# Attention queries turned once per pair and split behind the turn, in a two-layer hybrid backbone on one core

## The chip, the cores and the metric

The kernel runs on one core of one Trainium2 chip. The metric is the device time of one execution in microseconds (us), the median of three runs. One further execution was taken by the hardware profiler, and all rows below come from it.

## What is computed

Two layers of a hybrid backbone (pooling, attention, gated DeltaNet) run over 1,024 latent tokens and 128 context tokens. The change is in the attention, of which the reference says:

```
s = jnp.einsum('bqkgd,bskd->bkgqs', qblk, k, preferred_element_type=jnp.float32) * scale
p = jax.nn.softmax(s, axis=-1).astype(v.dtype)
return jnp.einsum('bkgqs,bskd->bqkgd', p, v)
```

There are 8 query heads of 64 channels and 2 key heads (4 query heads share one). Latent queries attend to 1,024 latent and 128 cached context keys, context queries to the 128 context keys alone. Each layer ends with the output projection of the gated branches, a norm and a residual.

## The kernel before

**Tiling.** `attention` works on nine pairs. Pair 0 is all context queries; pairs 1 to 8 are two heads by 512 latent queries (`PAIRS`). The inner loop has one step per pair and key tile of 128 keys, 73 steps in a layer (`ATTN_STEPS`): one for pair 0, nine for each other pair. `BASE[p]` is the first step of pair p: 0, 1, 10, 19, 28, 37, 46, 55, 64.

**A step.** TensorE computes the scores of the *next* step (`scores(n + 1)`: L1901 with the high part of the queries, `QH`, and L1902 with the low part, `QL`, for two heads), then the small items of the step's slot, then the weighted values of this step (`weighted_values`, L1911). ScalarE takes two exponentials per step (L1736), GpSimd adds them up (`add`, L1670).

**The split.** A query in float32 is a high part, rounded to float32r, and the remainder, the low part. Row 64 of `QL` holds a query's maximum over the keys and meets a row of -1 in `KO`, so that the scores come out with the maximum taken off.

**How queries get there.** A pair is handled in two halves ("asks"). For each, GpSimd's `split` copies the queries twice, rounded, into `qhh` (L1653) and subtracts to get `ql` (L1656). Item `hi`: TensorE turns (transposes) four blocks of `qhh` into PSUM bank 7 (L1811), and ScalarE copies them to `QH` (L1712). Items `max`: TensorE multiplies a block of 128 queries with all 1,152 keys (L1858, three products), VectorE reduces to a maximum per query, a column of `ql` (L1940), eight times per pair. Item `lo`: TensorE turns `ql` with its column of maxima (L1840), ScalarE copies it to `QL` (L1712). That is 16 turned blocks per pair.

**Bank 7** is also where the sums of exponentials land (`sum`, L1876) and where the DeltaNet output is turned (`o`, L1884). Each user waits until the one before has been read out (`turn_start`).

**The order** is written by hand. `attention_slots` puts the items in slots, one per step, and all engines follow it: `slots[23]` is done by each engine in step 23. Inside a slot `rank` sorts. `first` is what goes ahead of the loop, and the first four `hi` items ride in the DeltaNet scan (`QUERY_TURNS`: after scan steps 8, 10, 12, 14). VectorE also has `recip` (reciprocals, L1950), `norm` (L1958), `gate` (L1981, both inputs in SBUF), and `oscale` (scaling of `of`, L1990, both in SBUF). In the loop:

```
for n, items in enumerate(steps):
    if n + 1 < len(ATTN_STEPS):
        scores(n + 1)
    for item in items:
        work(item)
    weighted_values(n)
```

`project_out` loads the blocks of the output weights when the last `lo` is turned (six of them) and when the last scores are done (two).

## Time and profile before

| | us |
|---|---|
| median of three runs (1728.01 to 1728.64) | 1728.17 |
| the profiled execution | 1731.49 |
| its span on the core | 1729.7 |
| attention loop, layer 0, from the second score of step 1 to the first product of the projection | 580.0 to 793.0 |
| the same loop in layer 1 begins about 824 us later | |
| TensorE's mean granted clock, of full speed | 0.984 |

A row of the timeline gives the start and duration of an instruction or of a run of alike ones; "idle before" in brackets, with what ended it. Line numbers are of the kernel before. The start of the next row on an engine, less its own, is what an instruction costs there, since durations of pipelined products overlap.

### The profile page before, as it was taken

How to read it: one execution, taken by the hardware profiler on the slowest of the kernel's cores; microseconds unless marked ns; L12 is line 12 of the kernel's file. 1: busy time of each engine (PE TensorE's matmuls, PEld its weight loads, DVE VectorE, ACT ScalarE, POOL GpSimd, SP SyncE). 2: the span in 40 equal slices, each digit the busy share in tenths (PEclk: the TensorE clock that was granted, in tenths of full speed). 3: DMA queues.
4: the chain of work that ended last, by engine and by line, in shares of the span. 5: the costliest groups of instructions: out<-in, count | busy, mean ns of one | idle time of the engine just before them, and what ended most of it. 6: DMA issues, size and time to landing. Idle time of an engine off the chain costs nothing. (4 is left out here: it accounts for less than half of the span.)

```text
span 1729.7 us, 40122 instructions
## 1 busy us (share of the span) xinstructions
PE 1637.1 (95%) x17250; PEld 1343.1 (78%) x17250; DVE 1001.0 (58%) x1471; ACT 621.3 (36%) x1260; POOL 924.0 (53%) x854
## 2 busy tenths in 40 slices
PE   4899999989998999999999999998999899999998
PEld 2788999978997655556879999997899765555586
DVE  2664243827774777779238513382777477777911
ACT  4411231124444444455234123112444444445511
POOL 1000389029992587885320047911999358788532
PEclk9899999999999999999999999999999899999999
DMA  9345312210000000113321211231000000010422
GB/s 340 137 159 172 105 32 89 80 62 16 16 4 12 14 13 27 34 36 136 123 89 38 64 39 51 62 102 60 22 17 4 12 14 13 20 40 21 152 95 77
DMA packets 69776, 112.37 MB, mean 65 GB/s; under 512 B 9824, under 2 KB 41824, under 8 KB 69600
## 3 DMA queue, kind: packets, MB, share of 16 engines
q1 hardware_dynamic: 69136, 109.62, 18.8%
q8 instruction: 138, 2.26, 0.5%
q14 instruction: 38, 0.31, 0.1%
q10 hardware_dynamic: 464, 0.17, 0.0%
HBM read 90.30 MB, written 19.47 MB: 63 GB/s over the span
## 5 line engine op out<-in xcount | busy, mean ns | idle before, releaser
L1670 POOL TENSOR_TENSOR attn_accp<-attn_accp,attn_pr 128x1024 f32<-128x1024 f32 x110 | 269.4, 2449 | 42.9 <-ACT attn_pr L1736 37.2
L94 PE MATMUL ps<-in_h_hi,in_w_hi 128*128 128x384 f32 x720 | 244.1, 339 | 2.5 <-DVE in_h_lo L615 2.5
L96 PE MATMUL ps<-in_h_hi,in_w_lo 128*128 128x384 f32 x720 | 242.4, 337 | 0.0
L1940 DVE TENSOR_REDUCE attn_ql<-ps 128x1 f32<-128x1152 f32 x128 | 172.5, 1355 | 102.3 <-PE ps L1858 102.0
L1736 ACT ACTIVATE attn_pr<-ps 128x512 f32<-128x512 f32 x292 | 158.7, 595 | 170.7 <-PE ps L1902 161.8
L1901 PEld LDWEIGHTS ps<-attn_QH,attn_KH 128*128 128x128 f32 x292 | 55.5, 190 | 122.1 <-ACT attn_pr L1736 55.2
L94 PEld LDWEIGHTS ps<-in_h_hi,in_w_hi 128*128 128x128 f32 x720 | 135.7, 188 | 9.3 <-issue 7.5
L1911 PE MATMUL ps<-attn_pr,z 128*64 128x512 f32 x520 | 139.5, 615 | 0.0
L1144 POOL TENSOR_TENSOR delta_ML<-delta_EK,local 128x256 f32<-128x256 f32 x180 | 130.4, 746 | 15.2 <-PE ps L1184 14.5
L96 PEld LDWEIGHTS ps<-in_h_hi,in_w_lo 128*128 128x128 f32 x720 | 135.5, 188 | 0.0
L1901 PE MATMUL ps<-attn_QH,attn_KH 128*128 128x512 f32 x292 | 131.5, 450 | 0.0
L95 PE MATMUL ps<-in_h_lo,in_w_hi 128*128 128x384 f32 x384 | 129.6, 338 | 0.0
L94 PE MATMUL ps<-in_w_hi,in_h_hi 128*128 128x256 f32 (+1 forms) x432 | 124.2, 288 | 0.0
L1184 PE MATMUL ps<-delta_TR,delta_ML 64*64 64x64 f32 x2880 | 111.0, 223 | 13.7 <-POOL delta_ML L1144 7.9
L95 PE MATMUL ps<-in_w_lo,in_h_hi 128*128 128x256 f32 (+1 forms) x432 | 122.4, 283 | 0.0
L1902 PE MATMUL ps<-attn_QL,attn_KO 65*128 65x512 f32 x292 | 116.2, 398 | 0.0
L1184 PEld LDWEIGHTS ps<-delta_TR,delta_ML 64*64 64x64 f32 x2880 | 97.5, 137 | 20.8 <-DVE delta_TR L1430 11.7
L1430 DVE TENSOR_TENSOR delta_TR<-delta_TR,ps 128x256 f32<-128x256 f32 x180 | 72.7, 404 | 53.1 <-PE ps L1184 51.3
L1354 ACT ACTIVATE delta_X<-ps 128x256 f32<-128x256 f32 x180 | 68.8, 382 | 64.4 <-PE ps L1184 60.4
L1858 PE MATMUL ps<-attn_KH,attn_QH 128*128 128x384 f32 x384 | 89.6, 341 | 2.0 <-DVE attn_ql L1940 2.0
L1184 PE MATMUL ps<-delta_X,delta_TR 64*64 64x64 f32 x2304 | 86.4, 222 | 1.4 <-issue 0.7
L931 ACT ACTIVATE in_gate<-ps 128x384 f32<-128x384 f32 x48 | 23.4, 492 | 174.6 <-PE ps L96 93.7
(308 smaller groups left out, 3857.0 us busy)
## 6 DMA issues: line engine op xcount, KB each, us to landing
in_w<-in_w_in SPq DMA_DIRECT2D x21, 1024.0 KB, 5.1
z<-in_w_mod SPq DMA_DIRECT2D x8, 2048.0 KB, 8.0
gates<-in_gate SPq DMA_DIRECT2D x48, 192.0 KB, 1.9
attn_gt<-gates SPq DMA_DIRECT2D x34, 256.0 KB, 2.6
z<-in_x_sample SPq DMA_DIRECT2D x16, 512.0 KB, 6.0
zz<-in_w_mod SPq DMA_DIRECT2D x4, 2048.0 KB, 13.4
out_w<-in_w_out SPq DMA_DIRECT2D x16, 512.0 KB, 5.7
out_y<-z SPq DMA_DIRECT2D x16, 512.0 KB, 2.9
```

The lines of the kernel that those rows point to most:

```text
L94: nc.tensor.matmul(out, a_hi(i), b_hi(i), start=(i == 0), stop=False)
L95: nc.tensor.matmul(out, a_hi(i), b_lo(i), start=False, stop=False)
L96: last = nc.tensor.matmul(out, a_lo(i), b_hi(i), start=False, stop=(i == n - 1))
L1144: nc.gpsimd.tensor_tensor(pairs(ML[d][:, i % 2]), EA[d][:, j % 3, :, 0], level_mask(i, d), ALU.mult).then_inc(ml_done, 1)
L1184: last = nc.tensor.matmul(heads(bank, off)[rows(c), h, :], lhs(rows(c), h), rhs(rows(c), h), start=True, stop=True)
L1670: nc.gpsimd.tensor_tensor(acc, a, pr[:, n % 4], ALU.add).then_inc(pool_added, 1)
L1736: nc.scalar.activation(pr[:, n % 4, e], ps[:, e, :], ACT.Exp, scale=HD ** -0.5).then_inc(p_done, 1)
L1858: last = nc.tensor.matmul(ps[:, bank + c, 0:GRP], QH[:, p % 3, blk // 2, col:col + P], KH[:, g, GRP * c:GRP * c + GRP], start=True, stop=True)
L1901: nc.tensor.matmul(ps[:, e, :], KH[:, g, ks], QH[:, p % 3, e, :], start=True, stop=False)
L1902: nc.tensor.matmul(ps[:, e, :], KO[0:HD + 1, g, ks], QL[0:HD + 1, p % 2, e, :], start=False, stop=True).then_inc(st_done, 1)
L1911: nc.tensor.matmul(ps[HD * e:HD * e + HD, 2 + p % 2, :], values(p, kt, e), pr[:, n % 4, e], start=(kt == 0), stop=(kt == STEPS_OF[p] - 1)) ...
L1940: nc.vector.tensor_reduce(ql[:, a % 4, blk, HD:HD + 1], ps[:, bank:bank + 3, 0:GRP], AX_XY, ALU.max).then_inc(mx_read, 1)
```

## The change

- A pair's queries are turned once, as they lie, from `z` (item `turn`, four blocks of 128 by 128, both heads of the pair in one block). ScalarE rounds each head out of bank 7 into `QH` (`high`, half of the partitions each), then copies each half to the other half of the partitions (`double`). VectorE subtracts, bank 7 less `QH`, into `QL` (`lows`, two instructions of 64 by 512). These are spread over four slots: `turn` with the first `high`, `second`, `low` with the first `double`, and the second `double`.
- GpSimd's `split`, the buffers `qhh` and `ql`, and the items `hi` and `lo` are gone.
- The eight maxima of a pair are columns of a small tile `mx`. Item `row` turns all eight at once (128 by 8), ScalarE copies them to `mrow` (8 by 128) and issues a DMA from its own queue that writes them as one row of 1,024 into row 64 of `QL`. The first score of the pair waits for that DMA (`row_in`).
- In the scan there are two turns (after steps 8 and 13) and two `lows` on VectorE (after 11 and 17). Two `max` items of pair 2 move from the slots to between the scores of step 0 and of step 1.
- The `o` items 3 to 8 move from slots 14, 16, ..., 24 to slots 16 to 21.
- `QL` has three buffers in place of two, the SBUF layout moves with it, and seven blocks of the output weights are loaded once the scores of step 63 are done, the eighth after the last scores.

```diff
def attention_slots():
...
-    first += [("max", 1, 0, b) for b in range(4)] + [("max", 1, 1, 0), ("lo", 0, 0), ("max", 1, 1, 1), ("lo", 0, 1), ("max", 1, 1, 2),
-                                                     ("lo", 1, 0), ("max", 1, 1, 3), ("lo", 1, 1), ("hi", 2, 0)]
+    first = [("max", 0, 0, None), ("max", 0, 1, None)] + [("max", 1, 0, b) for b in range(4)]
+    first += [("row", 0), ("turn", 2), ("max", 1, 1, 0), ("max", 1, 1, 1), ("low", 2), ("max", 1, 1, 2), ("max", 1, 1, 3), ("row", 1)]
+    between = [("max", 2, 0, 0), ("max", 2, 0, 1)]
     slots = [[] for _ in range(len(ATTN_STEPS) + KT_LAT)]
     for p in range(2, len(PAIRS)):
         b = BASE[p]
         for i in range(4):
-            slots[b - 11 + i + (p == 2)].append(("max", p, 0, i))
+            if ("max", p, 0, i) not in between:
+                slots[b - 11 + i + (p == 2)].append(("max", p, 0, i))
             slots[b - 7 + i + (p == 2)].append(("max", p, 1, i))
-        slots[b - 8].append(("hi", p, 1))
-        slots[b - 6 + (p == 2)].append(("lo", p, 0))
-        slots[b - 2].append(("lo", p, 1))
+        slots[b - 3 + (p == 2)].append(("row", p))
         if p >= 3:
-            slots[b - 12].append(("hi", p, 0))
+            slots[b - 15].append(("turn", p))
+            slots[b - 14].append(("second", p))
+            slots[b - 13].append(("low", p))
+            slots[b - 13].append(("double", p, 0))
+            slots[b - 12].append(("double", p, 1))
     for p, b in enumerate(BASE):
         end = b + STEPS_OF[p] - 1
         at = end + (1 if p == 0 else 3)
@@ -1510,12 +1513,13 @@
         slots[at + 6].append(("gate", p))
     for t in range(NT):
         slots[5 + 2 * t].append(("oscale", t))
-        slots[8 + 2 * t].append(("o", t))
+        slots[8 + 2 * t if t < 3 else 13 + t].append(("o", t))
     for n, (k, i) in enumerate(EXTRA_GATES):
         slots[23 + 3 * n].append(("gate", k, i))
     slots[1].append(("osum",))
-    rank = {"max": 0, "recip": 2, "norm": 3, "gate": 3, "osum": 4, "oscale": 5, "hi": 6, "lo": 7, "sum": 8, "o": 9}
-    return first, [sorted(s, key=lambda x: rank[x[0]]) for s in slots]
+    rank = {"low": 0, "max": 1, "row": 2, "recip": 2, "norm": 3, "gate": 3, "osum": 4, "oscale": 5, "turn": 6, "second": 6, "double": 7,
+            "sum": 8, "o": 9}
+    return first, between, [sorted(s, key=lambda x: rank[x[0]]) for s in slots]
 
 
...
-    rc, QL = sb("rc", [P, 2, QB]), sb("QL", [P, 2, 2, QB], F32R)
-    qhh, ql, ck = sb("qhh", [P, 4, 4, P]), sb("ql", [P, 4, 4, HD + 2]), sb("ck", [P, NKV * HD])
+    QL = sb("QL", [P, 3, 2, QB], F32R)
+    mx, mrow, ck = sb("mx", [P, 3, 2, 4]), sb("mrow", [8, P], F32R), sb("ck", [P, NKV * HD])
+    row_in = [sem(f"row_in{i}") for i in range(3)]
+    for item in [("turn", 0), ("turn", 1)] + first + [x for s in slots for x in s]:
...
         sp.wait_ge(kv_out, 32)
 
     def gpsimd(pool):
-        def split(p, i):
-            n = ASKS.index((p, i))
-            if n >= 4:
-                is_turned(pool, "hi", *ASKS[n - 4])
-                is_turned(pool, "lo", *ASKS[n - 4])
-            q = queries(p, i)
-            if n < 4:
-                pool.wait_ge(q_high, n + 1)
-            for e in range(2 if n >= 4 else 0):
-                nc.gpsimd.tensor_copy(blocks(qhh[:, n % 4, :, HD * e:HD * e + HD], p).bitcast(F32R), q)
-            if n >= 4:
-                pool.drain()
...
             nc.scalar.activation(dst, src, ACT.Copy, scale=scale).then_inc(turn_copied, 1)
 
         def evict(item):
-            if item[0] == "hi":
-                _, p, i = item
-                copied(item, query_columns(QH[:, p % 3], p, i), turned_columns(slice(0, P), p))
-            elif item[0] == "lo":
-                _, p, i = item
-                r = slice(0, HD + 1)
-                copied(item, query_columns(QL[r, p % 2], p, i), turned_columns(r, p))
+            def high(p, e):
+                nc.scalar.activation(of_head(QH, half(e), p, e), turned_queries(p, e), ACT.Copy).then_inc(q_high, 1)
+
+            def double(p, e):
+                act.wait_ge(q_high, 2 * p + 2)
+                nc.scalar.activation(of_head(QH, half(1 - e), p, e), of_head(QH, half(e), p, e).bitcast(F32), ACT.Copy).then_inc(q_ready, 1)
+
+            if item[0] == "turn":
+                p = item[1]
+                is_turned(act, *item)
+                high(p, 0)
+                if p < 3:
+                    high(p, 1)
+                    double(p, 0)
+                    double(p, 1)
+            elif item[0] == "second":
+                high(item[1], 1)
+            elif item[0] == "double":
+                double(*item[1:])
+            elif item[0] == "row":
+                p = item[1]
+                is_turned(act, *item)
+                if p:
+                    act.wait_ge(row_in[(p - 1) % 3], 16 * ((p - 1) // 3 + 1))
+                nc.scalar.activation(mrow[:], ps[0:8, 7, 0:P], ACT.Copy).then_inc(turn_copied, 1)
+                act.wait_ge(turn_copied, turn[item] + 1)
+                act.dma_start(QL[HD:HD + 1, p % 3].rearrange("p e (t c) -> p (e t) c", c=P).bitcast(F32),
+                              mrow[:].bitcast(F32)).then_inc(row_in[p % 3], 16)
             elif item[0] == "sum":
                 p = item[1]
...
         if s in KEY_TURNS:
             key_turn(pe, KEY_TURNS.index(s))
         if s in QUERY_TURNS:
-            query_turn(pe, *ASKS[QUERY_TURNS.index(s)])
+            query_turn(pe, QUERY_TURNS.index(s))
+
+    def lows(dve, p):
+        dve.wait_ge(q_high, 2 * p + 2)
+        for e in range(2):
+            last = nc.vector.tensor_tensor(of_head(QL, slice(0, HD), p, e), turned_queries(p, e),
+                                           of_head(QH, half(e), p, e).bitcast(F32), ALU.subtract)
+        last.then_inc(turn_copied, 1)
+
+    def early_lows(dve, s):
+        if s in EARLY_LOWS:
+            lows(dve, EARLY_LOWS.index(s))
     def tensor(pe, out, nxt):
         def work(item):
-            if item[0] == "hi":
-                query_turn(pe, *item[1:])
-            elif item[0] == "lo":
-                _, p, i = item
-                n = ASKS.index((p, i))
+            if item[0] == "turn":
+                query_turn(pe, item[1])
+            elif item[0] == "row":
+                p = item[1]
                 turn_start(pe, item)
-                pe.wait_ge(mx_read, call_number[p, i, None if p == 0 else 3] + 1)
-                for blk in range(4):
-                    last = nc.tensor.transpose(ps[0:HD + 1, 7, P * blk:P * blk + P], ql[:, n % 4, blk, 0:HD + 1], m["ident"])
-                last.then_inc(turned, 1)
+                pe.wait_ge(mx_read, call_number[p, 1, None if p == 0 else 3] + 1)
+                nc.tensor.transpose(ps[0:8, 7, 0:P], mx[:, p % 3].rearrange("p e t -> p (e t)"), m["ident"]).then_inc(turned, 1)
             elif item[0] == "max":
                 _, p, i, blk = item
                 n, g = call_number[p, i, blk], i if p == 0 else PAIRS[p][1]
                 bank = call_bank(n)
-                is_turn_copied(pe, "hi", p, i)
+                pe.wait_ge(q_ready, 2 * p + 2)
                 if n < 2:
...
@@ -1893,13 +1890,14 @@
                 pe.wait_ge(ones_done, 1)
                 pe.wait_ge(k_copied, len(K_BANKS))
             if kt == 0:
-                is_turn_copied(pe, "lo", p, 1)
+                is_turn_copied(pe, "turn", p)
+                pe.wait_ge(row_in[p % 3], 16 * (p // 3 + 1))
             for e in range(2):
                 if n >= 1:
                     pe.wait_ge(p_done, 2 * (n - 1) + e + 1)
                 g = groups(p)[e]
                 nc.tensor.matmul(ps[:, e, :], KH[:, g, ks], QH[:, p % 3, e, :], start=True, stop=False)
-                nc.tensor.matmul(ps[:, e, :], KO[0:HD + 1, g, ks], QL[0:HD + 1, p % 2, e, :],
+                nc.tensor.matmul(ps[:, e, :], KO[0:HD + 1, g, ks], QL[0:HD + 1, p % 3, e, :],
                                  start=False, stop=True).then_inc(st_done, 1)
 
         def weighted_values(n):
...
-        for item in first[4:-1]:
+        for item in first:
-        work(first[-1])
+        for item in between:
+            work(item)
...
-QUERY_TURNS = (8, 10, 12, 14)
+QUERY_TURNS = (8, 13)
+EARLY_LOWS = (11, 17)
...
-        attn["queries_turned"](sp)
-        for k in range(6):
+        attn["last_pair_begun"](sp)
+        for k in range(KD - 1):
             w_block(k)
         attn["scores_done"](sp)
-        w_block(6)
-        w_block(7)
+        w_block(KD - 1)
         attn["values_done"](sp)
```

At three places the order on an engine is worth seeing. The first is VectorE from the end of the scan to slot 2 (`attn_ql` and `attn_mx` take the maxima, `attn_QL` is the low part), the change against before:

```order
-L1937 TENSOR_REDUCE attn_ql<-ps 128x4 x2
-L1940 TENSOR_REDUCE attn_ql<-ps 128x1 x10
+L1822 TENSOR_TENSOR attn_QL<-ps,attn_QH 64x512 x2
+L1934 TENSOR_REDUCE attn_mx<-ps 128x4 x2
+L1938 TENSOR_REDUCE attn_mx<-ps 128x1 x6
+L1822 TENSOR_TENSOR attn_QL<-ps,attn_QH 64x512 x2
+L1938 TENSOR_REDUCE attn_mx<-ps 128x1 x4
```

Two pairs of subtractions have come in, one ahead of the first maxima and one between the sixth and the seventh.

The second is TensorE around the scores of step 0, now (L1855 is the product for a maximum, L1899 and L1900 the scores):

```order
L1855 MATMUL ps<-attn_KH,attn_QH 128x384 x6
L1838 MATMUL ps<-masks,attn_mx 8x128
L1899 MATMUL ps<-attn_QH,attn_KH 128x512
L1900 MATMUL ps<-attn_QL,attn_KO 128x512
L1899 MATMUL ps<-attn_QH,attn_KH 128x512
L1900 MATMUL ps<-attn_QL,attn_KO 128x512
L1855 MATMUL ps<-attn_KH,attn_QH 128x384 x6
L1899 MATMUL ps<-attn_QH,attn_KH 128x512
```

The second L1855 row is the two moved `max` items; before, four turned blocks of `qhh` (L1811) stood there.

The third is VectorE in slots 22 to 24, the change against before (`pbr<-pbr,attn_gt` is the `gate` item of slot 23):

```order
 L1950 RECIPROCAL attn_rc<-attn_rc 128x128
 L1981 TENSOR_TENSOR pbr<-pbr,attn_gt 128x512
-L1940 TENSOR_REDUCE attn_ql<-ps 128x1
+L1822 TENSOR_TENSOR attn_QL<-ps,attn_QH 64x512 x2
+L1938 TENSOR_REDUCE attn_mx<-ps 128x1
 L1950 RECIPROCAL attn_rc<-attn_rc 128x128 x2
```

The subtractions of pair 5 now stand between the gate of slot 23 and the last maximum of pair 4. TensorE turns that pair's row in the next slot, 25; before, its last `lo` was in slot 26.

## Rows read from the trace of the kernel before

**Rows 1.** Windows; PE, PEld, DVE, ACT, POOL busy, PEclk, DMA share, GB/s.
```profile
680.00:792.96 112.96, 112.96 (x489) 59.05 (x485) 89.01 (x74) 60.55 (x112) 96.59 (x55) 1.00 0.17 55
```

**Rows 2.** Timeline of TensorE, layer 0: start us, duration us, line, operands, count.
```profile
691.49 0.50 PE L1901 MATMUL ps<-attn_QH,attn_KH 128*128 128x512 f32 x1
...
693.05 0.60 PE L1840 MATMUL ps<-masks,attn_ql 128*65 128x128 f32 x4
...
693.58 1.08 PE L1911 MATMUL ps<-attn_pr,z 128*64 128x512 f32 x4
...
694.59 0.50 PE L1901 MATMUL ps<-attn_QH,attn_KH 128*128 128x512 f32 x1
...
697.26 0.50 PE L1901 MATMUL ps<-attn_QH,attn_KH 128*128 128x512 f32 x1
```

**Rows 3.** Waits of TensorE, 582 to 792 us: total us, times, longest.
```profile
PE ps L1884 <- ACT attn_QH L1712: 1.4, 2, 0.8
PE ps L1884 <- ACT attn_QL L1712: 1.4, 2, 0.7
PE ps L1858 <- DVE attn_ql L1940: 1.0, 2, 0.6
PE ps L1811 <- POOL attn_ql L1656: 0.9, 1, 0.9
PE ps L1884 <- ACT attn_rc L1712: 0.7, 1, 0.7
```

**Rows 4.** Timeline of all engines, 655 to 667 us, steps 23 to 25.
```profile
657.43 0.69 PE L1858 MATMUL ps<-attn_KH,attn_QH 128*128 128x384 f32 x3
...
658.16 1.36 DVE L1940 TENSOR_REDUCE attn_ql<-ps 128x1 f32<-128x1152 f32 x1 [2.01 <-PE ps L1858]
...
658.33 2.38 POOL L1670 TENSOR_TENSOR attn_accp<-attn_accp,attn_pr 128x1024 f32<-128x1024 f32 x1 [0.31 <-ACT attn_pr L1736]
...
659.43 0.94 DVE L1950 RECIPROCAL attn_rc<-attn_rc 128x128 f32<-128x128 f32 x1
...
659.84 1.09 ACT L1736 ACTIVATE attn_pr<-ps 128x512 f32<-128x512 f32 x2 [1.59 <-PE ps L1902]
...
660.11 0.69 PE L1858 MATMUL ps<-attn_KH,attn_QH 128*128 128x384 f32 x3
...
660.29 0.96 DVE L1981 TENSOR_TENSOR pbr<-pbr,attn_gt 128x512 f32<-128x512 f32 x1
...
661.18 1.34 DVE L1940 TENSOR_REDUCE attn_ql<-ps 128x1 f32<-128x1152 f32 x1
...
663.00 0.60 PE L1811 MATMUL ps<-masks,attn_qhh 128*128 128x128 f32 x4
```

**Rows 5.** Timeline of VectorE: the start, and two scalings of `of`.
```profile
566.53 10.40 DVE L1940 TENSOR_REDUCE attn_ql<-ps 128x1 f32<-128x1152 f32 x8 [0.68 <-PE ps L1858]
...
606.67 2.58 DVE L1990 TENSOR_TENSOR of<-of,attn_oss 128x256 f32<-128x256 f32 x1
...
651.75 1.47 DVE L1990 TENSOR_TENSOR of<-of,attn_oss 128x256 f32<-128x256 f32 x1
```

**Rows 6.** Timeline of TensorE at the start of the step loop.
```profile
580.04 0.78 PE L1901 MATMUL ps<-attn_QH,attn_KH 128*128 128x512 f32 x1
...
583.05 0.50 PE L1901 MATMUL ps<-attn_QH,attn_KH 128*128 128x512 f32 x1
```

**Rows 7.** Groups by form: two evictions of a bank of 512 columns.
```profile
L1958 DVE TENSOR_TENSOR zz<-ps,attn_rc 128x512 f32<-128x512 f32 x16 | 10.9, 681 | 0.1
...
L1712 ACT ACTIVATE attn_QH<-ps 128x512 fp32r<-128x512 f32 x36 | 21.6, 599 | 14.7 <-PE ps L1811 14.7
```

**Rows 8.** ScalarE's timeline: its first transfer issued in the kernel.
```profile
5.15 0.39 ACTq L881 DMA_DIRECT2D rows<-in_rows  x1
```

**Rows 9.** DMA issues: engine, count, KB, median us to landing.
```profile
attn_gt<-gates SPq DMA_DIRECT2D x8, 64.0 KB, 1.7
```

**Rows 10.** The view of line 1626, transfers of 0.2 KB.
```profile
DMA to landing us min/median/max: 2.1/2.8/3.8
```

98 lines of the change are left out of this document (37 added, 61 removed).

## The prediction

> **What bounds the kernel now.** I read the windows of the attention loop first. In the second half of it TensorE is busy for 113 of 113 us, VectorE for 89 and GpSimd for 97, at the full granted clock [rows 1]. So there the time is what TensorE has to issue, and VectorE is the engine with the least room among those that TensorE waits for. The timeline gives the price of a step: from one first score to the next it takes 3.10 us with a block of four turned tiles in it (691.49 to 694.59) and 2.67 us without (694.59 to 697.26) [rows 2]. A block of four costs 0.43 us of the step, although it occupies TensorE for 0.53 (693.05 to 693.58) [rows 2]. The waits come third: in the loop of one layer TensorE stands still for 5.4 us in eight waits, most of them for bank 7, where an `o` item follows another user in the same slot [rows 3]. In layer 1 the loop has the same items, so I work out one layer and double it.
>
> **What goes.** Ahead of the change, slots hold 27 blocks of four: three for pair 2, four for each of pairs 3 to 8. Now there are six, the `turn` items of pairs 3 to 8. That is 21 x 0.43 = 9.0 us less. Seven `row` items (pairs 2 to 8) come in; one turned tile occupies a quarter of 0.53, and from nothing to 0.13 of it shows in a step, so I take 0.1 each, 0.7 us more. GpSimd loses `split`. I cost that at nothing: TensorE waited for it once, 0.9 us [rows 3], and this is in the next sum.
>
> **What waits now.** The 5.4 us of the old waits all fall away, since each belongs to an item that moved, and a new list takes their place. It follows from how VectorE stands to TensorE in a step [rows 4]. The product for a maximum starts at 657.43, the reduction at 658.16 for 1.36, the reciprocal at 659.43, the gate at 660.29. GpSimd's addition runs from 658.33 for 2.38, to 660.71, and the gate ends at 661.25, half a microsecond after it; the gate sits out the addition. The Trainium skill's page "SBUF — State Buffer", section "Who interferes with whom", says that a VectorE instruction with two SBUF inputs and a GpSimd instruction that reads SBUF exclude each other for their whole length, while one with a single SBUF input is not held; the trace agrees, the gate being of the first kind.
>
> A subtraction reads PSUM and SBUF as L1958 does, 0.681 us for 512 columns [rows 7], so a pair of them is about 1.3 us (neighbours overlap by some 0.08, as the starts in rows 4 show).
>
> - *The row waits, pairs 4 to 7.* The subtractions of the next pair stand behind a gate and ahead of the last maximum of this pair. From 661.25, 1.3 us of them and 1.36 of reduction end at 663.9. TensorE arrives for the row when the next step's scores are issued, at 662.7 (663.00 [rows 4] less some 0.3 for the `o` item that leaves slot 24). It waits 1.2 us. Four pairs have a gate there: 4.8 us. Before, the last `lo` was a slot later, and this had slack.
> - *Pair 3's row, slot 16.* No gate, but the reciprocal and a longer scaling ahead put the row 0.4 us late, and `o` 3 in the same slot waits 0.7 for bank 7 (the size of such a wait in rows 3): 1.1.
> - *`o` 8 in slot 21.* Its scaling is in the same slot. The scaling at 651.75 lasts 1.47 [rows 5] and starts some 2.0 after the product (1.36 of reduction behind the 0.73 until it starts), so `o` can go 3.6 us after the product's start, where TensorE arrives at about 1.5 (0.6 of product, 0.9 of `sum`): 2.1.
> - *Slot 12*, `sum` and `o` together as before: 0.7.
> - *Slots 3, 7 and 9.* VectorE has the sum of squares, then a scaling, the subtractions of pair 3, the norm of pair 0, a gate and a scaling of up to 2.58 us [rows 5]. Adding them up against TensorE's steps, the next product for a maximum, which needs the last one reduced, comes 0.9, 0.8 and 1.9 us late. This is the least certain entry.
>
> Together 12.3 us.
>
> **ScalarE** has two `high` and two `double` copies in place of four evictions, all near the 0.60 of L1712 [rows 7], and in each pair a small copy and the issue of a DMA, for which 0.39 us stands in the trace [rows 8]. In a step it is idle for 1.59 us [rows 4]. I cost it at nothing in the loop; without that cover it would be some 0.7 us per pair.
>
> **The row's DMA.** From the row on TensorE to the first score of the pair lie a weighted value (1.0), scores (1.0), a product (0.6) and a weighted value (1.0): 3.7 us. The copy takes some 0.5 with its handshake, the landing between 1.7 (64 KB [rows 9]) and 2.8 (the median for 0.2 KB [rows 10]): 2.2 to 3.3. It fits. For pair 2 the row is a slot later and only 1.4 us are left, so 0.8 to 1.9 us would show, but slot 9's wait for VectorE covers the same time; I add nothing and keep 1 us for the range. The Trainium skill's page "DMA: Bandwidth & Descriptors", section "Anatomy of one DMA — SWDGE (gpsimd) path", gives a fixed 2.0 us, fitted on GpSimd's queue; an estimate by it leaves the sum as it is.
>
> **The start of the loop.** The eight reductions of pair 1 run back to back from 566.53 for 10.40 us [rows 5], and the first score of step 1 follows at 580.04, that of step 2 at 583.05 [rows 6]. The subtractions of pair 2 stand between the sixth and the seventh maximum, on this path: +1.3. In the scan, two blocks go but one pair of subtractions enters VectorE's chain, where a scan step is adds and products in turn; I take +0.4 (from -0.9, the two blocks alone, to +1.0). The subtractions of pair 1 end the scan behind its last add and overlap TensorE's first product. Then, from the last reduction to the score of step 1, two blocks of 0.4 to 0.7 leave and two `max` items come in, the second of which needs the first reduced: 0.7 + 0.1 + 1.36 + 0.7, at the slower clock that the 0.78 us score at 580.04 shows against 0.50 at 583.05 [rows 6]. That is 2.9 + 0.1 - 1.1 = +1.9. Slots 0 and 1 lose these products, 2 x 0.55 = -1.1. Start: +2.5.
>
> **The end.** Seven blocks of weights start where six did, within the same step 62; nothing waits for the seventh. Nothing.
>
> **Sum** of a layer: -9.0 + 0.7 - 5.4 + 12.3 + 2.5 = +1.1 us, of two +2.2 us. Against the profiled execution of 1731.5 that is 1733.7; it stands 3.3 us above the median of the runs, 1728.2, and against that the forecast is 1730.4 us. A measurement of this kernel can tell about 0.2%, 3.5 us, from no change: my forecast is no change that can be told. TensorE does 16.6 us less, and gives it back in waits.
>
> **Rivals.**
>
> *A, faster: VectorE keeps up.* The list of waits is worked with each item at its latest. If the row waits are nil, `o` 8 finds its tile scaled and slot 9 is no later than before, 4.8 + 1.4 + 1.9 us go in each layer, 16 us in all: 1714 us; with half of it 1722. For it speaks that GpSimd, free of `split`, is out of VectorE's way more; against it that a gate behind a reduction and a reciprocal meets an addition in any case [rows 4].
>
> *B, slower: the row lands late.* The price turns on the landing. Up to 3.1 us it is hidden; at 3.8, the longest for 0.2 KB [rows 10], each of six pairs waits 0.7 and pair 2 some 2 us, 6.2 in a layer: 1743 us. Against it: 64 KB land in 1.7 [rows 9], and the medians lie below the point.
>
> *C, slower: VectorE is later than worked out.* GpSimd's addition also holds the subtractions, up to 2.4 us each time, and the four row waits become 3 us: +15, 1745 us. The 0.681 us of L1958 over 16 instructions, in a loop where GpSimd is nearly always busy, speak against it [rows 7]. By the skill's page on SBUF this cannot happen. A milder form, 0.7 us more at each of the four rows, gives 1736.
>
> *D, the start is cheaper or dearer* by 1.5 us a layer, 3 in all: inside the range.
>
> **Chances.** Forecast, within 3.5 us of 1728.2: 0.38. A: 0.30. B: 0.15. C in both forms with other waits that I did not see: 0.17, together 0.32 for slower. The forecast's own range is 1726 to 1735. To leave out no more than 2 in 10 the range takes in the near half of A and of B and C: 1718 to 1741.
>
> **What would show it.** Right: four-block turns fall from 288 to 72 tiles a kernel; TensorE shows waits of about 1.2 us for the last maximum ahead of the row at four pairs per layer, one of about 2 for `oscale` in slot 21, and one between the two maxima after step 0; a plain step stays at 2.67; the first score of step 1 comes some 3.6 us later (0.4 + 1.3 + 1.9), and the loop takes some 2.5 us less from there. Wrong: no waits ahead of the rows (A), first scores of a pair that wait for a DMA (B), subtractions longer than 0.7 (C).

## The result and the profile after

| | before | after |
|---|---|---|
| median, us (four runs each) | 1728.41 | 1741.89 |
| range of the runs, us | 1728.01 to 1729.33 | 1738.30 to 1744.62 |
| the profiled execution, us | 1731.49 | 1741.61 |
| TensorE busy in it, of the span | 1637.1 of 1729.7 | 1623.8 of 1739.8 |

The ratio is 1.0076, with a 95% interval of 1.0057 to 1.0095. The change is slower by 13.5 us. The forecast was 1730.4, and 1741.9 lies just above its range. The four runs of the change scatter by 6 us, the four of before by 1.3; that need not be the change's doing, since the 17 to 23 runs of before in each group of experiments below scatter by 6 to 10 us.

TensorE is busy for 13.3 us less and idle for 23.4 us more (116.0 against 92.6). So the work went, and more than that came back as waiting. The page of the profile after:

```profile
span 1739.8 us, 39560 instructions
...
PE 1623.8 (93%) x17052; PEld 1319.6 (76%) x17052; DVE 1015.8 (58%) x1507; ACT 624.7 (36%) x1262; POOL 876.2 (50%) x762
...
PEclk8999999999999999999999999999999989999999
...
L1938 DVE TENSOR_REDUCE attn_mx<-ps 128x1 f32<-128x1152 f32 x128 | 172.5, 1354 | 94.9 <-PE ps L1855 94.1
...
L1899 PE MATMUL ps<-attn_QH,attn_KH 128*128 128x512 f32 x292 | 133.1, 456 | 1.0 <-issue 0.8
...
L1855 PE MATMUL ps<-attn_KH,attn_QH 128*128 128x384 f32 x384 | 91.8, 349 | 8.8 <-DVE attn_mx L1938 8.8
...
```

The reductions (L1938) last 1354 ns each and the scores 456, as before within a few ns. L1855 has the products for a maximum. Nothing became slower by itself; I look for waits.

**Waits of TensorE in the loop.** This answers to [rows 3]: the loop of layer 0 from slot 2 on, each row a line of the kernel on TensorE, what it waited for, the sum, the count and the longest. Layer 1 has the same rows.

```profile
...
engine line waited for: us in total, times, longest us
PE ps L1838 <- DVE attn_mx L1938: 4.8, 5, 1.2
PE ps L1855 <- DVE attn_mx L1938: 2.9, 4, 1.5
PE ps L1881 <- DVE of L1990: 2.0, 1, 2.0
PE ps L1881 <- ACT attn_mrow L1722: 0.7, 2, 0.4
PE ps L1881 <- ACT attn_rc L1695: 0.7, 1, 0.7
PE ps L1899 <- issue: 0.4, 1, 0.4
```

L1838 turns the row of maxima, L1881 the DeltaNet output. The sum is 11.5 us against 5.4 before. This is nearly the forecast's list: 4.8 for the rows, 2.0 for `o` 8 behind its scaling, 2.9 for maxima that come late. The last entry is the first score of pair 2. It starts 1.87 us after the row's DMA was issued, as nearly all such scores do (e7 and e11 come back to it), so this is a wait for the landing, though the profile names no releaser.

**Steps.** The trace also gives each step's length, from one first weighted value (L1911 before, L1909 after) to the next; step n holds the items of slot n. In both kernels nearly every step is 2.14 us, plus 0.53 for a product for a maximum, 0.44 for a four-block turn, 0.91 for `sum`, 0.22 for `o` and nothing that can be read for `row`. What a step has above that I call its excess. Steps in us, layer 0 / layer 1:

| step | before | after | excess after | in it |
|---|---|---|---|---|
| 1 | 3.58 / 3.58 | 4.31 / 4.48 | 1.3 / 1.4 | half clock; TensorE has no wait in it |
| 8 | 4.22 / 4.22 | 4.05 / 4.05 | 1.1 | `o` 0 behind row 2 in bank 7 |
| 9 | 2.67 / 2.67 | 4.85 / 5.38 | 2.2 / 2.7 | late reduction, row's DMA, half clock |
| 10 | 2.89 / 2.89 | 2.89 / 3.77 | 0 / 0.9 | half clock |
| 21 | 3.58 / 3.58 | 6.31 / 6.07 | 2.5 / 2.3 | `o` 8 behind its scaling |
| 22 | 4.17 / 4.17 | 4.37 / 3.12 | 1.3 / 0 | half clock |
| 25, 34, 43, 52 | 2.58 | 3.58 | 1.4 each | row behind gate, subtractions, last maximum |

Steps 3, 12 and 16 have an excess of 1.0 each, 7 of 0.6 and 20 of 0.3. From the first weighted value to the last, the items now add up to 192.5 us in a layer against 202.2, and the excess to 18.0 (18.1 in layer 1) against 6.8. The sums are those of the trace: 210.46 and 210.57 us against 209.06 and 209.05, +1.4 and +1.5.

**The row's wait in close-up**, which answers to [rows 4] (slots 24 and 25, layer 0; start, duration, engine, line, what it writes and reads, idle before and what ended it):

```profile
...
663.37 0.69 PE L1855 MATMUL ps<-attn_KH,attn_QH 128*128 128x384 f32 x3
663.56 0.96 DVE L1981 TENSOR_TENSOR pbr<-pbr,attn_gt 128x512 f32<-128x512 f32 x1
...
664.26 2.51 POOL L1663 TENSOR_TENSOR attn_accp<-attn_accp,attn_pr 128x1024 f32<-128x1024 f32 x1 [0.29 <-ACT attn_pr L1740]
664.45 1.38 DVE L1822 TENSOR_TENSOR attn_QL<-ps,attn_QH 64x512 fp32r<-64x512 f32 x2
...
665.86 1.36 DVE L1938 TENSOR_REDUCE attn_mx<-ps 128x1 f32<-128x1152 f32 x1
...
667.37 0.27 PE L1838 MATMUL ps<-masks,attn_mx 128*8 128x128 f32 x1 [1.16 <-DVE attn_mx L1938]
...
667.67 0.27 ACT L1722 ACTIVATE attn_mrow<-ps 8x128 fp32r<-8x128 f32 x1 [0.82 <-PE ps L1838]
667.97 0.63 ACTq L1724 DMA_DIRECT2D attn_QL<-attn_mrow  x1
...
```

The gate (L1981) is done at 664.45, the two subtractions (L1822) at 665.86, the reduction at 667.25, and TensorE, which came 1.16 us earlier, turns the row at 667.37. The order on VectorE is the forecast's. The subtractions last 0.69 us beside GpSimd's addition; their median over all 36 is 0.688 us and the longest 0.694. The 24 in the loops run beside an addition, the 12 ahead of the loops do not, and both kinds last the same. By the Trainium skill's page "SBUF — State Buffer", section "Who interferes with whom", an instruction with a single SBUF input is not held by GpSimd: the trace agrees.

**The start of the loop**, layer 1 (the answer to [rows 5, 6]):

```profile
...
1400.01 1.21 ACT L1699 ACTIVATE attn_QH<-ps 64x512 fp32r<-64x512 f32 x2 [0.75 <-PE ps L1800]
...
1401.25 1.28 ACT L1703 ACTIVATE attn_QH<-attn_QH 64x512 fp32r<-64x512 f32 x2
...
1402.99 0.71 PE L2285 MATMUL ps<-masks,gcol 128*128 128x128 f32 x4 [1.53 <-ACT zz L2180]
1403.19 1.39 DVE L1822 TENSOR_TENSOR attn_QL<-ps,attn_QH 64x512 fp32r<-64x512 f32 x2
...
1404.61 2.62 DVE L1938 TENSOR_REDUCE attn_mx<-ps 128x1 f32<-128x1152 f32 x2
...
1407.38 0.27 PE L1838 MATMUL ps<-masks,attn_mx 128*8 128x128 f32 x1 [2.63 <-DVE attn_mx L1938]
...
1407.72 0.60 PE L1899 MATMUL ps<-attn_QH,attn_KH 128*128 128x512 f32 x1
...
1408.12 0.63 PE L1900 MATMUL ps<-attn_QL,attn_KO 65*128 65x512 f32 x1
...
1409.40 1.16 PE L1855 MATMUL ps<-attn_KH,attn_QH 128*128 128x384 f32 x3
...
1412.10 1.30 PE L1855 MATMUL ps<-attn_KH,attn_QH 128*128 128x384 f32 x3 [1.54 <-DVE attn_mx L1938]
...
1414.29 0.60 ACT L1740 ACTIVATE attn_pr<-ps 128x512 f32<-128x512 f32 x1 [4.06 <-PE ps L1900]
...
1415.04 1.98 PE L1909 MATMUL ps<-attn_pr,z 128*64 128x512 f32 x4
...
```

Four things are seen. ScalarE has four copies for the turn of pair 2 in a row (1400.01 to 1402.53), and behind them a copy of the projection's (L2180) for which TensorE waits 1.53 us. The subtractions stand between reductions, and VectorE is busy without a pause until the last reduction ends at 1407.23, so TensorE waits 2.63 us ahead of row 1; its earlier wait of 1.53 us only makes this one shorter (in layer 0 the late product costs VectorE 0.26 us). Then it waits 1.54 us between the two maxima. And from 1407.9 on it runs at half speed: a score takes 0.63 us in place of 0.40, a weighted value 1.98 in place of 1.08. The windows show the granted clock (busy time of PE, PEld, DVE, ACT, POOL with counts, then the clock of full speed, DMA share, GB/s):

```profile
...
1401.00:1406.00 5.00, 2.22 (x13) 1.58 (x11) 4.92 (x6) 2.25 (x5) 0.00 (x0) 1.00 0.00 2
1406.00:1411.00 5.00, 3.11 (x8) 2.04 (x8) 1.64 (x2) 1.46 (x3) 0.00 (x0) 0.69 0.03 6
1411.00:1416.00 5.00, 3.90 (x11) 2.42 (x11) 2.31 (x2) 1.20 (x2) 0.00 (x0) 0.50 0.00 0
1416.00:1421.00 5.00, 5.00 (x18) 2.09 (x15) 0.63 (x1) 1.71 (x3) 1.61 (x1) 0.78 0.00 0
...
```

TensorE was busy for 2.22 of the 5 us from 1401, and the clock falls to its lower level, 1.2 of 2.4 GHz, for about 10 us. Before, the same stretch of layer 1 ran at 1.00 throughout; in layer 0 it fell there too, for about 3.5 us (the 0.78 us score of [rows 6]).

The first score and the second weighted value of the same stretch before (the first product for a maximum starts at 1389.13):

```profile
...
1403.06 0.47 PE L1901 MATMUL ps<-attn_QH,attn_KH 128*128 128x512 f32 x1
...
1409.78 1.03 PE L1911 MATMUL ps<-attn_pr,z 128*64 128x512 f32 x4
...
```

The account in sums, of profiled execution against profiled execution: from the first product for a maximum to the second weighted value +4.8 and +7.3 us (26.87 and 27.97 against 22.10 and 20.65), from there to the last weighted value +0.7 and +0.6. Together +13.4. The remaining -3.3 us lie ahead of the loops and behind them, most of it ahead of layer 0's, where the profiled execution of before took longer; it stands 3.3 us above its median. These stretches differ from one execution to the next without any edit to them: over the 12 traces of the change and the versions made from it, the kernel's start to the first product for a maximum takes 559.1 to 565.1 us, and the last weighted value of layer 0 to that product in layer 1 takes 595.2 to 601.4. So a difference of a few us between two executions can be theirs, and below I read gains from the steps as well as from the medians.

### The profile page after: what moved, and what is told of

Read it like the earlier page. It is cut to its first block and busy times, and to the rows that moved or that the text cites. A ratio compares the mean times of both kernels' runs of the same rounds, so it can differ in the third digit from the quotient of the medians.

```text
span 1739.8 us, 39560 instructions
## 1 busy us (share of the span) xinstructions
PE 1623.8 (93%) x17052; PEld 1319.6 (76%) x17052; DVE 1015.8 (58%) x1507; ACT 624.7 (36%) x1262; POOL 876.2 (50%) x762
## 5 line engine op out<-in xcount | busy, mean ns | idle before, releaser
L1663 POOL TENSOR_TENSOR attn_accp<-attn_accp,attn_pr 128x1024 f32<-128x1024 f32 x110 | 265.9, 2418 | 62.8 <-ACT attn_pr L1740 59.3
L1938 DVE TENSOR_REDUCE attn_mx<-ps 128x1 f32<-128x1152 f32 x128 | 172.5, 1354 | 94.9 <-PE ps L1855 94.1
L1740 ACT ACTIVATE attn_pr<-ps 128x512 f32<-128x512 f32 x292 | 158.9, 595 | 174.8 <-PE ps L1900 167.1
L1899 PEld LDWEIGHTS ps<-attn_QH,attn_KH 128*128 128x128 f32 x292 | 56.3, 193 | 126.7 <-ACT attn_pr L1740 60.1
L1909 PE MATMUL ps<-attn_pr,z 128*64 128x512 f32 x520 | 142.3, 626 | 0.0
L1899 PE MATMUL ps<-attn_QH,attn_KH 128*128 128x512 f32 x292 | 133.1, 456 | 1.0 <-issue 0.8
L1900 PE MATMUL ps<-attn_QL,attn_KO 65*128 65x512 f32 x292 | 117.7, 403 | 0.0
L1855 PE MATMUL ps<-attn_KH,attn_QH 128*128 128x384 f32 x384 | 91.8, 349 | 8.8 <-DVE attn_mx L1938 8.8
L1855 PEld LDWEIGHTS ps<-attn_KH,attn_QH 128*128 128x128 f32 x384 | 70.2, 193 | 22.7 <-issue 13.7
## 6 DMA issues: line engine op xcount, KB each, us to landing
zz<-in_w_mod SPq DMA_DIRECT2D x4, 2048.0 KB, 13.4
```

Of the source, the lines that this page charges most:

```text
L1663: nc.gpsimd.tensor_tensor(acc, a, pr[:, n % 4], ALU.add).then_inc(pool_added, 1)
L1740: nc.scalar.activation(pr[:, n % 4, e], ps[:, e, :], ACT.Exp, scale=HD ** -0.5).then_inc(p_done, 1)
L1855: last = nc.tensor.matmul(ps[:, bank + c, 0:GRP], QH[:, p % 3, blk // 2, col:col + P], KH[:, g, GRP * c:GRP * c + GRP], start=True, stop=True)
L1899: nc.tensor.matmul(ps[:, e, :], KH[:, g, ks], QH[:, p % 3, e, :], start=True, stop=False)
L1900: nc.tensor.matmul(ps[:, e, :], KO[0:HD + 1, g, ks], QL[0:HD + 1, p % 3, e, :], start=False, stop=True).then_inc(st_done, 1)
L1909: nc.tensor.matmul(ps[HD * e:HD * e + HD, 2 + p % 2, :], values(p, kt, e), pr[:, n % 4, e], start=(kt == 0), stop=(kt == STEPS_OF[p] - 1)) ...
```

## The experiments

All but one start from the change, and each was timed in five rounds beside the kernel before (4 to 12 runs each). They ran in three groups, e1 to e4, e5 to e8 and e9 to e12, each on a chip of its own; the medians of before are 1727.8, 1728.1 and 1728.8. Where the intervals of two kernels overlap, their medians alone do not order them.

| kernel | median, us | ratio to before (95%) |
|---|---|---|
| the change | 1741.9 | 1.0076 (1.0057 to 1.0095) |
| e1 gates a slot earlier | 1732.4 | 1.0028 (1.0017 to 1.0039) |
| e2 scaling of tile 8 a slot earlier | 1738.5 | 1.0063 (1.0050 to 1.0077) |
| e3 maxima back in slots 0, 1 | 1736.0 | 1.0049 (1.0036 to 1.0062) |
| e4 waits at the start filled | 1739.9 | 1.0074 (1.0060 to 1.0088) |
| e5 start rebuilt | 1732.0 | 1.0018 (1.0005 to 1.0031) |
| e6 scalings on ScalarE | 1732.5 | 1.0028 (1.0016 to 1.0041) |
| e7 row 2 ahead of its maximum | 1743.5 | 1.0091 (1.0074 to 1.0109) |
| e8 e1, e2, e5, e6, e7 together | 1716.3 | 0.9932 (0.9916 to 0.9949) |
| e9 before, scalings on ScalarE | 1728.8 | 1.0001 (0.9988 to 1.0013) |
| e10 e8, wait ahead of row 1 filled | 1713.4 | 0.9910 (0.9896 to 0.9923) |
| e11 e10, `o` 0 to 2 in slots 9 to 11 | 1711.1 | 0.9897 (0.9882 to 0.9912) |
| e12 e8, row sent as two DMAs | 1722.4 | 0.9963 (0.9951 to 0.9975) |

**e1: the gates out of the way.**

```diff
-        slots[23 + 3 * n].append(("gate", k, i))
+        slots[22 + 3 * n].append(("gate", k, i))
```

> The change, with the twelve extra gates one slot earlier (22, 25, 28, ... in place of 23, 26, 29, ...), so that no gate stands ahead of the last maximum of pairs 4 to 7. Theory G (the row waits come from VectorE's order gate, subtractions, last maximum; in the trace of the change the steps 25, 34, 43 and 52 are 1.4 us longer than their items): these four steps fall from 3.57 to about 2.2 us, in two layers 8 x 1.3 = 10.5 us, 1731 us against 1742. Rival H (the subtractions are held by GpSimd's additions, so the gate does not matter): the waits stay above 1 us and the time within 2 us of the change. Rival K (the gates in slots 22, 25, 28 make other reductions late): the steps 25, 34 shrink, but 22 to 24 grow by as much.

Steps 25, 34, 43 and 52 fall from 3.57 to 2.64 us, eight times 0.93, which is 7.4 of the 9.5 us of the medians. No other step grows by the edit: the stretch at half clock in steps 9 and 10 is in layer 0 here and in layer 1 in the change, and step 1 takes 4.53 and 3.42 us in place of 4.31 and 4.48, again with the clock. The waits for the row go from 4.8 to 1.1 us in a layer (waits of TensorE in the loop of e1, from slot 2 on):

```profile
...
engine line waited for: us in total, times, longest us
...
PE ps L1838 <- DVE attn_mx L1938: 1.1, 5, 0.2
...
```

Theory G holds, H and K fall. The steps stay 0.4 us longer than the 2.2 expected; half of it is the 0.2 us that TensorE still waits each time.

**e2: the scaling of tile 8.**

```diff
-        slots[5 + 2 * t].append(("oscale", t))
+        slots[min(5 + 2 * t, 20)].append(("oscale", t))
```

> The change, with the scaling of tile 8 in slot 20 in place of slot 21, a slot ahead of its turn. Theory: step 21 loses its 2.3 to 2.5 us of wait but for at most 0.5, and with it goes the stretch at the lower granted clock behind it (0.60 in layer 0, where step 22 was 1.26 us too long): 4 to 6 us in two layers, 1737 against 1742. Rival: VectorE has no room in slots 19 and 20, the wait moves to slot 21's product for a maximum, and under 2 us are won.

Step 21 goes from 6.31 and 6.07 to 4.89, 2.6 us in two layers. Step 22 of layer 0 goes from 4.37 to 3.12 at full clock, but it does so in e1, e3 and e4 too, which leave it alone. The intervals overlap; the steps show the gain. The median moves by 3.4 us, a little less than expected, since 1.1 us of step 21 stay: `o` 8 then waits for the copy of the sum in bank 7. The forecast named one wait there; there were two.

**e3: the maxima of pair 2 back in slots 0 and 1.**

```diff
-    between = [("max", 2, 0, 0), ("max", 2, 0, 1)]
+    between = []
```

> The change, with the first two maxima of pair 2 back in slots 0 and 1. Theory S (the start lost more than was forecast since TensorE stands still between the maxima, 1.54 us, and again in slot 1, 1.3 us, and runs there at the lower granted clock): 3 to 4 us a layer, 6 to 8 in all, 1735 against 1742; the weighted value of step 0 takes about 1.1 us in place of 1.98, or the low clock at least ends earlier. Rival P (the price is what the forecast had, +1.9 between the scores and -1.1 in the slots): 1.6 us in all, 1740.

The median is 5.9 us lower, just under S's 6 to 8, and the intervals overlap a little. But the trace does not find the gain where S has it. The second weighted value comes 27.5 and 25.9 us after the first product, against 26.9 and 28.0: 0.6 us later in layer 0 and 2.0 sooner in layer 1, 1.4 in all, which is P's 1.6. Another 2.7 us of the trace are steps 9, 10, 21 and 22, which run at full clock here and which the edit does not touch. So e3 does not decide between S and P. The start still falls to half clock, in layer 1 right behind the wait of 2.62 us ahead of row 1, and step 1 takes 5.2 and 4.7 us. With no product between the scores, the score of step 1 waits for the landing of row 1's DMA (layer 0 and layer 1):

```profile
...
578.62 0.76 PE L1899 MATMUL ps<-attn_QH,attn_KH 128*128 128x512 f32 x1 [0.97 <-ACT attn_pr L1740]
...
1409.17 0.76 PE L1899 MATMUL ps<-attn_QH,attn_KH 128*128 128x512 f32 x1 [0.61 <-DMA attn_QL<-attn_mrow]
...
```

They start 1.89 and 1.85 us after the DMA was issued. In layer 0 the profile names the exponentials (L1740), a pair of 1.09 us that begins at 577.46. By the code this score needs only the first of the two, which was over by about 578.0, and the row. The two moved maxima had covered this.

**e4: idle work in the waits.**

```diff
+    def fill(pe, count):
+        pe.wait_ge(grow_done, 8)
+        for _ in range(count):
+            nc.tensor.matmul(ps[:, 3, 0:P], m["ident"], m["ident"], start=True, stop=True)
...
         for item in first:
+            if item == ("row", 1):
+                out["fill"](pe, 16)
...
         for item in between:
             work(item)
+            if item == between[0]:
+                out["fill"](pe, 8)
...
```

> The change, with idle work for TensorE in its waits at the start of the loop: 16 products of 128 by 128 ahead of row 1 (about 2 us, where it waits 2.6) and 8 between the two maxima of pair 2 (about 1 us, where it waits 1.54), into a bank that nobody reads then. Nothing else differs. Theory C (the granted clock falls to half because TensorE stands still, and this adds to the waits): the stretch from the first score to the second weighted value runs at 1.00 and takes 2 to 3 us less a layer, 4 to 6 in all, 1737 against 1742. Rival N (the time there is VectorE's chain alone, or the clock falls in any case): within 1 us of the change.

The start runs at 1.00 in both layers, and the second weighted value comes 1.7 and 3.4 us sooner (25.1 and 24.6 us after the first product), although the idle work delays the first score by 0.8 and 0.5 us. From the first score to the second weighted value it takes 7.9 us in both layers in place of 10.5 and 11.8. So the low clock there costs 2.6 and 3.9 us beyond the waits: theory C holds. And step 1, in layer 1, has its weighted values 3.05 us apart:

```profile
...
1417.33 1.08 PE L1909 MATMUL ps<-attn_pr,z 128*64 128x512 f32 x4
...
1420.38 1.03 PE L1909 MATMUL ps<-attn_pr,z 128*64 128x512 f32 x4
...
```

That is 0.53 us less than the 3.58 before: without its product, and at full clock, the step is as much shorter as the forecast had it.

The time does not show the gain. The median moves by 2 us, the ratio (1.0074) not at all, and the profiled execution is 1.0 us longer than the change's. The loops from the second weighted value on are as long as there (206.1 to 206.2 us in each layer): steps 9 and 10 of layer 0 take 5.30 and 4.00 us in place of 4.85 and 2.89 and step 10 of layer 1 4.46 in place of 3.77, all at half clock, but step 22 of layer 0 is back at full clock. The 6.0 us that hide the gain lie outside the loops, in stretches that the edit leaves alone. Whether the median would show it with more runs stays open.

**e5: the start rebuilt.** Pair 2 is turned into bank 3, its subtractions follow the last maximum of pair 1, and slots 0 and 1 have their maxima.

```diff
-    first += [("row", 0), ("turn", 2), ("max", 1, 1, 0), ("max", 1, 1, 1), ("low", 2), ("max", 1, 1, 2), ("max", 1, 1, 3), ("row", 1)]
-    between = [("max", 2, 0, 0), ("max", 2, 0, 1)]
+    first += [("row", 0), ("max", 1, 1, 0), ("max", 1, 1, 1), ("max", 1, 1, 2), ("turn", 2), ("max", 1, 1, 3), ("low", 2), ("row", 1)]
+    between = []
...
-        x = ps[half(e), 7, :]
+        x = ps[half(e), 3 if p == 2 else 7, :]
...
```

What is left out gives this turn semaphores of its own and makes it wait until bank 3 is free.

> The change, with its start rebuilt: pair 2 is turned into bank 3, which is free once the last spread is copied, so that its subtractions can follow the last maximum of pair 1 without holding bank 7, and the first two maxima of pair 2 are in slots 0 and 1. Theory S (the start lost 4 to 7 us a layer: subtractions in VectorE's chain of reductions, a pause while row 0 and the turn are done, waits between the maxima): the first score comes some 2 us sooner than in the change (14.2 against 16.2 to 16.4 us after the first product for a maximum), and the second weighted value 4 to 5 us sooner (22 to 23 us against 27 to 28): 8 to 10 us in all, 1732 to 1734 against 1742. Rival: something else in the start holds the first score (ScalarE's copies, the row's DMA), and it stays above 16.

The first score comes 13.8 us after the first product (16.2 to 16.4 in the change), the second weighted value after 22.8 and 23.0 us, 4.0 and 5.0 sooner. The median falls by 9.9 us, as expected; the start has 9.0 of it in the trace. From the second weighted value on a layer takes 204.8 us in place of 206.1 to 206.2, with no step at half clock, which is not the edit's doing. What is left of the loss at the start is 1.7 us of wait ahead of row 1, the half clock behind it, and in layer 0 1.0 us of wait for the landing of the row's DMA.

**e6: the scalings on ScalarE.**

```diff
...
-                nc.vector.tensor_tensor(o, o, oss[:, t].unsqueeze(2).broadcast_to([P, 4, HD]), ALU.mult).then_inc(o_ready, 1)
...
+                for h in range(4):
+                    o = of[:, t, HD * h:HD * h + HD]
+                    last = nc.scalar.activation(o, o, ACT.Copy, scale=oss[:, t, h:h + 1])
+                last.then_inc(o_ready, 1)
```

> The change, with the nine scalings of the DeltaNet output on ScalarE (four instructions of 128 by 64 each) in place of VectorE. Theory V (the waits of slots 9 and 21 are VectorE's scalings, stretched by GpSimd's additions): step 9 falls from 4.85 or 5.38 to about 3.2 us, where the wait of 0.5 us for the row's DMA stays, and step 21 from 6.07 to about 4.5; with the stretches at the lower clock that follow them 3.5 to 4 us a layer, 7 to 8 in all, 1734 against 1742. Rival D (step 9 waits for the row's DMA and not for VectorE): step 9 keeps over 4.3 us. Rival Q (ScalarE has no room): its exponentials come later and other steps grow.

Step 9 falls to 3.1 us, step 21 to 4.87, step 7 by 0.4 and step 20 by 0.3; no step grows. The median moves by 9.4, more than expected; 1.8 us of the trace's gain lie at the start, which the edit leaves alone and where the clock was up again sooner (step 1 takes 3.49 and 3.44 us). Theory V holds, D and Q fall.

**e7: row 2 ahead of its maximum.**

```diff
-    rank = {"low": 0, "max": 1, "row": 2,
+    rank = {"row": -1, "low": 0, "max": 1,
```

> The change, with the row ranked ahead of the maximum in its slot; only pair 2 has both in one slot (8), so its row leaves TensorE some 0.6 us earlier in each layer and nothing else moves. Theory D (in step 9 the first score of pair 2 waits about 0.5 us for the row's DMA, 1.87 us from issue to score, and then 1.5 for the reduction that VectorE has late): the wait ahead of the score goes and the reduction's wait grows by about as much, so the time stays within 1 us of the change. Rival: the DMA sets the step, and 1 us or more goes in two layers.

Step 8 is 0.55 shorter, step 9 1.1 longer in layer 0 and 0.6 in layer 1. TensorE in slots 8 and 9, layer 1:

```profile
...
1439.74 0.27 PE L1838 MATMUL ps<-masks,attn_mx 128*8 128x128 f32 x1 [0.24 <-DVE attn_mx L1938]
...
1440.78 1.08 PE L1909 MATMUL ps<-attn_pr,z 128*64 128x512 f32 x4
1442.20 0.47 PE L1899 MATMUL ps<-attn_QH,attn_KH 128*128 128x512 f32 x1 [0.35 <-issue]
...
1445.51 1.30 PE L1855 MATMUL ps<-attn_KH,attn_QH 128*128 128x384 f32 x3 [2.12 <-DVE attn_mx L1938]
1446.74 1.98 PE L1909 MATMUL ps<-attn_pr,attn_cv 128*64 128x512 f32 x4
...
```

The wait ahead of the first score stays at 0.35 us where D had it gone: the DMA is issued at 1440.34 and the score starts 1.86 us behind it, as it does in the change (1441.18 and 1443.05), so it came earlier by what the row did. TensorE stands longer for the reduction, 2.12 us, the clock falls (a weighted value of 1.98 us), and step 10 of layer 1 takes 5.24 us in place of 3.77. The median is 1.6 us above the change's, over D's 1 us; the two intervals overlap, so it is no gain and perhaps a loss. The rival falls: what comes early in front of a late reduction wins nothing.

**e8: all of it.** The five diffs together.

> All of it together on the change: gates one slot earlier, the scaling of tile 8 in slot 20, the start rebuilt, the scalings on ScalarE, the row of pair 2 ahead of its maximum. If the causes are separate, their gains add up, the scaling of slot 21 counted once: 8 + 8 to 10 + 7 to 8, 1742 less 23 to 26 is 1716 to 1719, below the kernel before by 9 to 12. Rival: VectorE or ScalarE has the same slack in several of them, or the granted clock falls in another place instead, and less than 18 are won, 1724 or more.

1716.3 us, inside the expectation. The gains of e1, e5 and e6, 9.5 + 9.9 + 9.4 = 28.8, and e7's loss give 27 if nothing overlaps (e2's is in e6's, since both empty slot 21); 25.6 were measured. So little of them overlaps, within the scatter of the medians. A layer's loop (first to last weighted value) takes 201.1 to 201.5 us in place of 210.5, and the combined kernel beats the one before by 0.7%.

On the page of e8 TensorE is busy for 1617.6 of 1712.0 us. It is idle for 94.4 us now, about as before the change (92.6), and works 19.5 us less.

**e9: is the gain the change's own?** The diff of e6, on the kernel before.

> The kernel before, with the nine scalings of the DeltaNet output on ScalarE in place of VectorE; nothing of the change. It tells how much of the gain of the combined version belongs to the old order too. Theory F (the scalings cost the change 7 to 9 us because its order puts them ahead of waits): before has 1.12 us too much in step 7 and part of the 0.89 in step 8 from them, so 1 to 2 us a layer go, 2 to 4 in all, 1724 to 1726 against 1728. Rival: it gains 7 or more here too, 1721 or less, and the combined version owes the change little.

No gain at all: step 7 keeps its 4.23 us and step 8 its 4.22. Both the theory, which gave these steps to the scalings, and its rival fall. The excess there must be another's (most waits of [rows 3] are for bank 7; no run tests it), and the scalings were hidden in the old order. So the part of e6 in e8 repairs the change's own order.

**e10: the last wait at the start filled.**

```diff
+                for _ in range(14 if p == 1 else 0):
+                    nc.tensor.transpose(ps[:, 7, 0:P], query_block(2, 0), m["ident"])
                 pe.wait_ge(mx_read, call_number[p, 1, None if p == 0 else 3] + 1)
```

> The combined version, with 14 turned tiles of idle work (about 1.8 us) in bank 7 ahead of row 1, where TensorE stands still for 1.77 us; nothing else differs. Theory C (the clock falls to half because TensorE stands still there, and step 0 and step 1 then run at half): the weighted value of step 0 takes 1.1 us in place of 1.94, and 1.5 to 2.5 us go in each layer, 3 to 5 in all, 1712 against 1716. Rival: the clock falls later instead, as in step 10 of the change with filled waits, and at most 1 us goes.

The loop runs at full clock throughout. The second weighted value comes after 21.3 and 20.9 us (22.8 and 23.1 in e8), step 1 is 3.57. The start gains 1.6 and 2.2 us in the trace, and no stretch of the loops is slow in its stead: theory C again. The median moves by 2.9 us, just under what was expected, and the intervals touch.

**e11: no `o` behind another user of bank 7.**

```diff
-        slots[8 + 2 * t if t < 3 else 13 + t].append(("o", t))
+        slots[9 + t if t < 3 else 13 + t].append(("o", t))
```

> As the combined version with the filled wait, and the o items of tiles 0 to 2 in slots 9, 10 and 11 in place of 8, 10 and 12, so that none follows another user of bank 7 in its slot. Theory: step 8 loses 0.6 (its wait behind the row) and step 12 1.0 us (its wait behind the sum), 1.5 us a layer, 3 in all against the version without it, 1709. Rival: step 9 or 11 grows by as much, since the waits there are ScalarE's.

Step 12 falls from 4.83 to 3.57 and step 8 from 3.50 to 3.28; steps 9 and 11, which take the items over, rise by 0.4 and 0.2. About 0.8 us a layer: less than expected but of that kind. The medians differ by 2.3, with intervals that overlap. The profiled execution shows something else at the score of step 1 in layer 0, where code and order are those of e10. The row's DMA and the score in the timeline of e11:

```profile
...
575.68 0.67 ACTq L1735 DMA_DIRECT2D attn_QL<-attn_mrow  x1
...
578.44 0.76 PE L1916 MATMUL ps<-attn_QH,attn_KH 128*128 128x512 f32 x1 [2.03 <-DMA attn_QL<-attn_mrow]
...
```

The same two rows of the timeline of e10:

```profile
...
576.64 0.67 ACTq L1735 DMA_DIRECT2D attn_QL<-attn_mrow  x1
...
578.51 0.47 PE L1916 MATMUL ps<-attn_QH,attn_KH 128*128 128x512 f32 x1 [1.17 <-ACT attn_pr L1751]
...
```

In e11 it starts 2.76 us after the row's DMA was issued, in e10 1.87. The profile names the exponentials (L1751) in e10, but as in e3 they were further on than the score needs, and 1.87 us is the usual distance: in the traces with one DMA to a row, 31 scores follow a wait and come within 4 us of its issue, and 30 of them start 1.84 to 1.89 us after it. The one in e11 is the exception. It waits 2.03 us for the landing, after which the clock fell and step 1 took 5.35 us. So a landing of this DMA is not always 1.9 us long.

**e12: the row as two DMAs.**

```diff
-                act.dma_start(QL[HD:HD + 1, p % 3].rearrange("p e (t c) -> p (e t) c", c=P).bitcast(F32),
-                              mrow[:].bitcast(F32)).then_inc(row_in[p % 3], 16)
+                for e in range(2):
+                    act.dma_start(QL[HD:HD + 1, p % 3, e].rearrange("p (t c) -> p t c", c=P).bitcast(F32),
+                                  mrow[4 * e:4 * e + 4].bitcast(F32)).then_inc(row_in[p % 3], 16)
...
-                pe.wait_ge(row_in[p % 3], 16 * (p // 3 + 1))
+                pe.wait_ge(row_in[p % 3], 32 * (p // 3 + 1))
...
```

> The combined version, with the row of maxima sent as two DMAs of 2 KB in place of one of 4 KB: ScalarE's queue issues twice (0.63 us each in the trace) and the first score of each pair waits for both. Theory D (the landing is hidden at pairs 3 to 8, where 3.7 us lie between row and first score, and ScalarE has room): only the first score of pair 2 and that of pairs 0 and 1 come later, by 0.6 us or less each, 0 to 3 us in all. Rival B (the landing or the issue is on the path at every pair): 0.6 us at each of 16 pairs, 8 us or more, 1724.

6.0 us more than e8, between the two. Steps 26, 35, 44 and 53 take 3.06 us in place of 2.66, eight times 0.4, step 9 0.25 more in each layer, and the second weighted value comes 1.0 us later in layer 0. These are not the pairs' first scores but the steps right behind a row. ScalarE and TensorE in slots 25 and 26:

```profile
...
663.83 1.22 ACTq L1736 DMA_DIRECT2D attn_QL<-attn_mrow  x2
...
664.44 0.50 PE L1915 MATMUL ps<-attn_QH,attn_KH 128*128 128x512 f32 x1
...
665.10 0.63 ACT L1704 ACTIVATE attn_QH<-attn_QH 64x512 fp32r<-64x512 f32 x1 [1.29 <-issue]
...
665.63 1.05 ACT L1752 ACTIVATE attn_pr<-ps 128x512 f32<-128x512 f32 x2
...
666.50 1.08 PE L1927 MATMUL ps<-attn_pr,z 128*64 128x512 f32 x4
...
```

The two issues (1.22 us in ScalarE's queue) and the `double` behind them push the exponentials (L1752) to 665.63, 1.19 us after the score; in e8 they start 0.77 us after it. The landing is hidden at these pairs, the issue is not: with one DMA ScalarE has just enough room, with two it has not. Theory D had ScalarE with room; rival B had named the issue, but at the first score of every pair, and it is the step behind the row at four pairs of a layer.

## Why the prediction was wrong

**The steps' prices held.** 0.43 us for a four-block turn: the fit over all steps gives 0.44. The `row` at 0.1: nothing to be read. A plain step stays at 2.67. GpSimd's part at nothing: no wait of TensorE for it is left in the loop.

**The row waits held.** 1.2 us at pairs 4 to 7 were forecast, 1.16 measured, by the order worked out (gate, subtractions, reduction). The steps are 1.4 us too long, 0.24 more than the wait, and 0.93 of that goes with the gates (e1). `o` 8: 2.1 forecast, 2.0 measured.

**The start failed.** This is the largest part. The forecast had +1.3 and +1.9 us, less 1.1 for slots 0 and 1: +2.1 in a layer. Measured were +4.8 and +7.3, 7.9 us too little in two layers. Two things were missing in that step.

First, the first score comes 2.4 and 2.2 us later after the first product for a maximum (16.4 and 16.2 us against 14.0 and 13.9), and the sum has 1.3 for it. The subtractions were priced (1.39 us), but row 0 and the turn of pair 2 on TensorE also stop VectorE's chain for 0.86 us (its idle time ahead of the reductions at 1400.54; 0.87 in layer 0, with another 0.26 ahead of the last two). That is all of it. I had costed ScalarE "at nothing in the loop" and had not asked about the stretch ahead of it; its four copies in a row make TensorE wait 1.53 us there, but row 1 waits for VectorE anyway, so this adds nothing in layer 1 and the 0.26 us in layer 0. That part is 2.1 us of the 7.9.

Second, and most of it, I took the low clock of [rows 6] as given and not as something that the change would bring about. From the first score to the second weighted value it takes 10.5 and 11.8 us, and 7.9 in both layers at full clock with the same products in it (e4): half clock costs 2.6 and 3.9 us. Before, the stretch took 8.1 us in layer 0, where the clock fell, and 6.7 in layer 1 and in both layers of e9, whose start is that of before. So the low clock there costs 5.0 us more in two layers than before. At full clock the moved products cost 7.9 - 6.7 = 1.2 us, where the forecast had 1.9 - 1.1 = 0.8, and step 1 is shorter by the forecast's 0.53 (e4); it is longer by 0.7 and 0.9 us in the change for the clock alone. The rebuilt start gave back 4.0 and 5.0 us (e5).

**The list of waits in the loop was short by some 2 us a layer.** From slot 2 on the forecast amounts to -1.4 us (-9.0 + 0.7 - 5.4 + 12.3), the trace to +0.7 and +0.6. Missing were `o` 0 behind row 2 in slot 8 (1.1; the same kind as the pairs that I did list in slots 12 and 16), and what half clock adds to steps 9, 10 and 22 (0.5, 0.9 and 1.3, each in one layer). Other entries were 0.2 to 0.3 small. Against them the old waits cost more than I took off ([rows 3] has 5.4 us of standstill, the steps an excess of 6.8), and the `row` items cost nothing. The half clock is the larger part of the 2 us here too: in e3 and e5, whose order from slot 2 on is the change's, these steps run at full clock, and the layer takes 204.7 to 204.8 us from the second weighted value on in place of 206.1 to 206.2, 0.7 less than before. That the profiled execution of the change had these stretches is chance.

**The DMA.** "It fits" was right for pairs 3 to 8: no first score of theirs waits. For pair 2 the wait is 0.4 us, and the product behind that score stands for 1.5 us more for VectorE: covered, as forecast. From issue to score it takes 1.87 us (layer 1: 1441.18 to 1443.05), less than the 2.2 us of copy and landing at best that the forecast had. Rival B was right in one point: where only scores cover the landing, as at row 1 in e3, e5, e8, e10 and e11, up to 1.2 us of it show, and 2.0 in e11 once. The issue takes 0.63 us on ScalarE, not the 0.39 of [rows 8].

**The rivals.** A had no case here: all its waits came. Its sum has 1.4 us for a tile scaled in time where the list of waits has 2.1, which makes it 1713 and not 1714. C was excluded rightly. None said that waits would lower the clock and so cost more than their length, nor that both ends of the start could be wrong on the same side. The range gave the start 1.5 us a layer, and it needed 4. The step that failed is thus the clock: it was left out of the sum, as a price for waits, at the start and in the loop.

Two layers: 7.9 + 4.1 = 12.0 us too little, less 0.8 that I gave the scan and that the trace does not show: 11.2 of the 11.5 us between 1730.4 and 1741.9. That this closes so well is partly luck, since the stretches ahead of the loops, the scan among them, differ by 6 us between executions; the 0.8 for the scan cannot be judged at all.

## What to carry to other kernels

Add up the items of each slot and compare with the trace: a step of 2.14 + 0.53 + 0.44 + 0.91 + 0.22 explains most of the 142 steps of two layers, and what is left over names the wait or the low clock. Work that leaves a place also leaves a gap: see what it covered (the landing of the row's DMA in e3), and whether TensorE's clock falls in it, since then the products behind it last twice as long. When a change saves work and loses time, repair its order before giving it up: this one went from +13.5 to -17.7 us against its control with gates, scalings and `o` items moved, a free bank for one turn, and a filled wait. And read a gain in the steps that the edit touches, in both layers: a profile of e3 or e4 taken whole says something else than its start.

## What was new of the hardware

- The granted clock fell to half after waits of 1.5 and 2.6 us at the start of layer 1, and in slot 9 after waits of 0.4 and 1.5 us; the latter in layer 1 and not in layer 0, with the same order. Idle work in the waits at the start kept it at 1.00 there (e4, e10). The same order can have such a fall in one execution and not in another: the start of layer 0 has it before and not in e9, steps 9 and 10 have it in layer 1 in the change, in layer 0 in e1, in both in e4 and in neither in e3 and e5.
- What makes runs of one kernel scatter is open. It is not this alone: the profiled execution of e12 has half clock at the start of both layers, and its five runs lie within 1.2 us, while the runs of before lie up to 10 us apart. The clock has a share in it outside the loops too. Ahead of layer 0's loop, the traces with a stretch of half clock between 530 and 545 us take 561.1 to 565.1 us up to the first product for a maximum, those without one 559.1 to 562.5.
- A DMA of 4 KB from SBUF to one row of SBUF, issued by ScalarE, takes 1.84 to 1.89 us from its issue to the score that waits for it, 30 times of 31, and once 2.76. It takes 0.63 us of ScalarE's queue.
- A subtraction with one input in PSUM and one in SBUF lasts 0.62 to 0.69 us, the 24 times beside one of GpSimd's additions as the 12 times without.
